# Two halves of weights taken together in up, gate and the first down, and other places for modulation rows 64 to 140

## The reference, cut to what matters

```
mod = silu(c) @ w_ada + b_ada                 # 6 slices of 2048: shift, scale, gate, twice
h = rms_norm(x, g) * (1 + scale_m) + shift_m
proj = h @ w_in                               # q, k, v, xs, z, b, c, dt
x = x + gate_m * (concat(attn, ssm) @ w_out)  # causal attention beside a state space mixer
h = rms_norm(x, g) * (1 + scale_f) + shift_f
u = causal_conv3(h @ w_up)                    # "up", 11264 columns
x = x + gate_f * ((silu(g) * val) @ w_down)   # "down", 5632 rows; then a final norm
# second block: norms, neighbourhood attention, latent attention, memory attention, and
x = x + (silu(h @ w_gate) * (h @ w_up)) @ w_down   # "gu" and "down2"
```

## Time and profile before

| | |
|---|---|
| median of 3 runs | 2675.37 us (2675.3 to 2676.28) |
| the profiled execution | 2672.84 us, its span 2670.9 us |
| mean granted TensorE clock | 0.996 of full |
| PE busy | 2625.8 us (98%) |
| POOL busy | 2197.8 us (82%) |
| ACT busy, DVE busy | 1252.9 us (47%), 1178.4 us (44%) |
| L1308 and L1313, PE busy | 833.8 us in 3328 matmuls, 464.7 us in 3328 matmuls |
| moved by DMA | 587.40 MB, 220 GB/s over the span |

### The profile page before, as it was taken

The page is one execution under the profiler, slowest core; times in us unless marked ns, Lnnn a source line. Parts: engine busy times, 40 slices in busy tenths (PEclk is TensorE's granted clock), DMA queues, the critical chain, the costliest instruction groups (busy, mean ns, idle before and its releaser), DMA issues.

```text
span 2670.9 us, 41760 instructions
## 1 busy us (share of the span) xinstructions
PE 2625.8 (98%) x16042; PEld 2349.0 (88%) x16042; DVE 1178.4 (44%) x1416; ACT 1252.9 (47%) x1496; POOL 2197.8 (82%) x889
## 2 busy tenths in 40 slices
PE   8999999999999999999999999999999999999998
PEld 8989998898888888888898888989998888888886
DVE  6777767774546464422364346722311111113223
ACT  5444454545444444444653454533544444444444
POOL 7878866787999998899898755866888888889997
PEclk9999999999999999999999999999999999999999
DMA  9998986674666665455455533634545555555553
GB/s 374 392 401 321 391 332 255 240 262 163 244 228 240 231 236 189 173 204 189 173 189 198 184 139 115 238 137 158 190 179 187 187 187 188 189 187 191 196 195 126
DMA packets 101760, 587.40 MB, mean 220 GB/s; under 512 B 11240, under 2 KB 13416, under 8 KB 45200
## 3 DMA queue, kind: packets, MB, share of 16 engines
q1 hardware_dynamic: 93600, 570.07, 57.7%
q10 hardware_dynamic: 8048, 15.74, 1.7%
HBM read 579.46 MB, written 8.40 MB: 220 GB/s over the span
## 4 chain that ended last, share of the span: by engine, by line
PE 85%; POOL 5%; DVE 4%; issue 3%; DMA 2%; ACT 1%; POOLq 0%; DVEq 0%; ACTq 0%; SPq 0%
PE ps L1308 29%; PE ps L1313 15%; PE ps L1325 6%; PE ps L1274 5%; PE ps L1267 5%; PE ps L1269 5%; POOL w_lo L547 5%; PE ps L1356 4%; PE ps L1358 4%; PE ps L1364 4%; PE ps L1330 3%; DMA arena<-ada 1%; DVE ps L2055 1%; PE ps L1631 1%; PE ps L1965 1%
## 5 line engine op out<-in xcount | busy, mean ns | idle before, releaser
L547 POOL TENSOR_TENSOR w_lo<-raw,w_hi 128x1024 fp32r<-128x1024 f32 x884 | 2197.4, 2500 | 455.2 <-ACT w_hi L570 452.5
L570 ACT CAST w_hi<-raw 128x1024 fp32r<-128x1024 f32 x884 | 924.3, 1051 | 1124.7 <-PE ps L1313 572.7
L1308 PE MATMUL ps<-a_both,w_hi 128*128 128x512 f32 x3328 | 833.8, 393 | 0.0
L1308 PEld LDWEIGHTS ps<-a_both,w_hi 128*128 128x128 f32 x3328 | 599.5, 189 | 106.1
L1313 PEld LDWEIGHTS ps<-a_both,w_lo 128*128 128x128 f32 x3328 | 454.0, 191 | 33.0 <-POOL w_lo L547 0.8
L1313 PE MATMUL ps<-a_both,w_lo 128*128 128x256 f32 x3328 | 464.7, 283 | 0.0
L1267 PE MATMUL ps<-a_both,w_hi 128*128 128x256 f32 x1616 | 404.9, 289 | 9.9 <-issue 3.3
L1269 PE MATMUL ps<-a_both,w_hi 128*128 128x256 f32 x1616 | 397.8, 284 | 0.0
L1267 PEld LDWEIGHTS ps<-a_both,w_hi 128*128 128x128 f32 x1616 | 311.7, 193 | 13.7 <-issue 4.8
L1269 PEld LDWEIGHTS ps<-a_both,w_hi 128*128 128x128 f32 x1616 | 312.0, 193 | 0.4
L2586 DVE TENSOR_TENSOR ps<-ps,work 128x1024 f32<-128x1024 f32 x42 | 51.8, 1232 | 505.9 <-ACT work L936 505.9
(11 more groups left out here) (262 smaller groups left out, 2034.6 us busy)
## 6 DMA issues: line engine op xcount, KB each, us to landing
raw<-stream SPq DMA_DIRECT2D x440, 1024.0 KB, 4.8
arena<-ada SPq DMA_DIRECT2D x185, 512.0 KB, 6.4
work<-ada SPq DMA_DIRECT2D x7, 512.0 KB, 7.1
arena<-memT SPq DMA_DIRECT2D x4, 512.0 KB, 10.0
res<-xT SPq DMA_DIRECT2D x4, 512.0 KB, 13.7
v_spill<-arena ACTq DMA_DIRECT2D x4, 512.0 KB, 3.4
k_spill<-arena ACTq DMA_DIRECT2D x4, 512.0 KB, 7.5
rel_rows<-rel_row ACTq DMA_DIRECT2D x4, 512.0 KB
```

Of the source, the lines that this page charges most:

```text
L547: pool.tensor_tensor(w_lo[:, h % SLOTS], raw_half(h), w_hi[:, h % SLOTS].bitcast(F32), ALU.subtract).then_inc(lo_ready, 1)
L570: act.copy(w_hi[:, base % 4], raw[:, tile_slot, (base % 2) * HALF:(base % 2 + 1) * HALF]).then_inc(hi_ready, 1)
L1308: pe.matmul(acc_two(g + turned)[:, f], w_hi[:, h % SLOTS, cols(k, f)], a_both[:, c0 + k], start=first and k == 0, stop=False, skip_group_c ...
```

## The change

It does two things that do not touch each other. `half_two` becomes `two_halves`: highs of half h, highs of half h + 1, then lows of h, lows of h + 1, with the same waits and the same count after each half's lows. Every caller goes in steps of two. The number of matmuls, weight loads and waits is the same. `ROW_POINTS` has other points between h = 62 and h = 140, so that VectorE's calls get these ends:

| call at h | 63 | 69 | 75 | 85 | 87 | 97 | 105 | 115 | 116 | 118 | 120 | 121 | 123 | 125 | 131 | 133 | 138 |
|---|---|---|---|---|---|---|---|---|---|---|---|---|---|---|---|---|---|
| rows until, before | 64 | 70 | 77 | 89 | 92 | 103 | 112 | 116 | 117 | 119 | 121 | 122 | 124 | 126 | 132 | 134 | 140 |
| rows until, after | 65 | 72 | 82 | 93 | 96 | 106 | 112 | 117 | 118 | 121 | 124 | 125 | 127 | 130 | 136 | 137 | 140 |

SyncE uses the same function, so that rows are issued behind other tiles: row 111 behind tile 54 and not 56, and rows 114 and 115 behind tile 56 and not 57.

```diff
--- before.py
+++ after.py
@@ -183,8 +183,8 @@
 
 
 
-ROW_POINTS = [(-1, 0), (3, 2), (58, 64), (62, 64), (66, 67), (92, 98), (105, 112), (111, 112), 
-              (138, 140), (146, 140), (164, 150), (168, 154), (176, 160), (186, 160)]
+ROW_POINTS = [(-1, 0), (3, 2), (58, 64), (62, 64), (66, 68), (69, 72), (75, 82), (92, 102), (103, 112), (111, 112),
+              (120, 124), (130, 136), (138, 140), (146, 140), (164, 150), (168, 154), (176, 160), (186, 160)]
 
 
 ADA_BACK = 150
@@ -1297,22 +1297,26 @@
                                        start=False, stop=last and k == 1, skip_group_check=True)
                 mm.then_inc(half_used, 1)
 
-            def half_two(h, g, c0, first, last, i=None, step=0, turned=0):
+            def two_halves(h, g, c0, first, last, i=None, step=0, turned=0):
 
                 def cols(k, f):
                     return slice(k * 512 + f * P, k * 512 + (f + 1) * P)
 
-                wait_high(h, i, step)
-                for k in range(2):
-                    for f in range(4):
-                        pe.matmul(acc_two(g + turned)[:, f], w_hi[:, h % SLOTS, cols(k, f)], a_both[:, c0 + k],
-                                  start=first and k == 0, stop=False, skip_group_check=True)
-                wait_half(h, i, step)
-                for k in range(2):
-                    for f in range(4):
-                        mm = pe.matmul(acc_two(g + turned)[:, f, 0, :], w_lo[:, h % SLOTS, cols(k, f)],
-                                       a_hi[:, c0 + k, :], start=False, stop=last and k == 1, skip_group_check=True)
-                mm.then_inc(half_used, 1)
+                for s in range(2):
+                    wait_high(h + s, i, step)
+                    for k in range(2):
+                        for f in range(4):
+                            pe.matmul(acc_two(g + turned)[:, f], w_hi[:, (h + s) % SLOTS, cols(k, f)],
+                                      a_both[:, c0 + 2 * s + k], start=first and s == 0 and k == 0, stop=False,
+                                      skip_group_check=True)
+                for s in range(2):
+                    wait_half(h + s, i, step)
+                    for k in range(2):
+                        for f in range(4):
+                            mm = pe.matmul(acc_two(g + turned)[:, f, 0, :], w_lo[:, (h + s) % SLOTS, cols(k, f)],
+                                           a_hi[:, c0 + 2 * s + k, :], start=False, stop=last and s == 1 and k == 1,
+                                           skip_group_check=True)
+                    mm.then_inc(half_used, 1)
 
             def half_pair(h, G, c0, first, last):
 
@@ -1344,8 +1348,8 @@
                 G, h0 = G0[name] + g, H0[name] + 8 * g
                 n = G // 2
                 pe.wait_ge(evac[G % 2], n if i is None else i + n)
-                for s in range(8):
-                    half_two(h0 + s, g, 2 * s, s == 0, s == 7, i, 16, int(name == "gu"))
+                for s in range(0, 8, 2):
+                    two_halves(h0 + s, g, 2 * s, s == 0, s == 6, i, 16, int(name == "gu"))
 
             def half_N(h, out2, c0, first, last, i=None, step=0):
 
@@ -1706,7 +1710,7 @@
                     G = G0["up"] + 20
                     pe.wait_ge(evac[G % 2], G // 2 + 1)
                     ada_sum(5, 0)
-                half_two(H0["up"] + 168 + s, 21, 2 * s, s == 0, s == 7)
+                two_halves(H0["up"] + 168 + s, 21, 2 * s, s == 0, s == 6)
 
             def down(name, hs0):
 
@@ -1731,7 +1735,8 @@
                         if first and kp == 0 and half == 1 and name == "down":
                             pe.wait_ge(evac[sets[cg]], (G + cg) // 2 + 1)
                         if name == "down":
-                            half_two(base_n + s, cg, par * 4 + 2 * kp, first and kp == 0, last and kp == 1, i, 8)
+                            if kp == 0:
+                                two_halves(base_n + s, cg, par * 4, first, last, i, 8)
                         else:
                             half_N(base_n + s, outs_tok[half][cg], par * 4 + 2 * kp, first and kp == 0,
                                    last and kp == 1, i, 8)
@@ -1765,9 +1770,7 @@
                             pe.wait_ge(mod_ready, len(ADA_ORDER))
                         for n in range(2):
                             pe.wait_ge(hl_ready, hs0 + n + 1)
-                            for kp in range(2):
-                                h = base + 4 * cg + 2 * n + kp
-                                half_two(h, cg, n * 4 + 2 * kp, n == 0 and kp == 0, False)
+                            two_halves(base + 4 * cg + 2 * n, cg, n * 4, n == 0, False)
 
                 for half in range(2):
                     n0 = 11 * half
```

## The result

The changed kernel takes 2687.02 us (median of 5 runs, 2685.24 to 2689.63) where the kernel before takes 2675.37 (5 runs): 1.0050 times as long, 95% interval 1.0038 to 1.0061, 11.6 us slower. The forecast was 2670.8 with a range to 2679; it was wrong in size and in sign. The profiled execution has a span of 2683.3 us, 12.4 more than before; it is the fastest of the five.

The account below looks back on a forecast made before the run. TensorE, busy 98% of the span, was taken as the bound, so only its waits or matmul pace could yield time. Pairs at -4.6 us and row terms summing to 0.0 turned 2675.37 into 2670.8 us, range 2659 to 2679.

Parts of the forecast that it names:

- Part one: Pairing halves in up, gu and down: each of 208 pairs saves 0.022 us net, -4.6 us.
- third rival: Order is free: pairing halves gains nothing and the row changes net 0, giving 2675.4 us; chance 0.12.
- I cost it at nothing: Later release of each pair's first half was priced at zero; 5.5 us over three places if the cover went.
- (a): Row 64 between two steps of the first norm, before the casts xs waits for: +0.5 us (0 to 1.3).
- (b): Three more rows and a fold before the second convolution of xs: +3.3 us, plus +1.7 for low clock.
- (c): TensorE's wait for VectorE at the dt sums disappears: -2.3 us (-2.3 to 0).
- (d): Seventh fold: row 111 issued sooner removes TensorE's wait, -2.4 us, and transposes stay at full clock, another -1.7.
- (f): Seventh pair of heads: one row less before `mixing` 13 removes the wait and its low clock, -3.9 us.
- (e): At the heads, more rows before `mixing` 5 make TensorE wait: +4.8 us (0 to +9.1).
- second rival: VectorE falls behind: at the heads more rows than fit between two pairs, +3.6 us, 2679.0 us; chance 0.13.

Follow-up runs that it names:

- experiment 8: Kernel before with two_halves and old row points, but up's last eight halves taken singly with half_two: 2667.82 us, 0.9981.
- experiment 5: Kernel before with the new row points only up to h = 87 (rows 64 to 96): 2676.64 us, 1.0011.
- experiment 6: Kernel before with row 111 one tile sooner and rows 130 and 131 ahead of `mixing` 11: 2667.90 us, 0.9980.
- 9: Kernel before with one row point edited, (105, 112) to (103, 112), putting rows 114 and 115 ahead of tile 57: 2679.21 us, 1.0020.
- experiment 1: Kernel before with two_halves alone, row points as before: 2671.46 us, 0.9993.
- experiment 10: Kernel before with new row points at 120 and 130 only, plus (116, 117) so row 116 stands behind `mixing` 2: 2680.01 us, 1.0024.
- experiment 3: Changed kernel, but SyncE issues rows 114 and 115 behind stream tile 57 again: 2679.85 us, 1.0026 against the kernel before.
- experiment 4: Kernel before with only the two new row points at 120 and 130, rows up to 112 as before: 2679.92 us, 1.0026.
- experiment 7: Kernel before with turned halves (highs h, lows h, lows h + 1, highs h + 1) in gu and up except its last group: 2669.31 us, 0.9987.
- experiment 2: Kernel before with the new row points alone, half_two as before: 2691.04 us, 1.0066.

## Why the prediction was wrong

**Part one, -4.6 forecast.** The pattern was right: a rise from 256 to 512 columns costs, a wait does not. In the kernel after only the first five of 16 highs are slow. A pair saves 0.020 us and not 0.022 (0.100 per five pairs, all through up and gu; the second low, too, is fast only behind a high, 0.119), so -4.2. The third rival, that the order is free, is out. The formula of the Trainium skill (TensorE: Matmul & The Clock Gate, Back-to-back issue gap) for the isolated gap of a matmul at full clock, columns over 2.4 GHz plus 2.5 ns, gives 216 and 109 ns for the two kinds (an estimate), and the same section has about 131 ns for 512 columns in a stream of weight loads and matmuls, which this is. The trace agrees with none of these figures: it has 227 and 120 in every kernel here. The failed step is "I cost it at nothing" for the later release. I looked only at the casts of w_hi and at w_lo in the first down. The cost came through other work in ScalarE's order, the casts of u, at the one place where a chain behind them ends on TensorE: 1.5 us, about the 1.85 us delay less the 0.5 us of room that L2087 had before; experiment 8, with single halves in that one group, has no such wait. A smaller slip: the 2.4 us for w_lo do not stand in the earlier trace rows, which have 2.8 each; with 2.8 the chain is 8.6 us and still far under 14.8.

**(a)** +0.5 forecast, 0.0 measured. With row 64 there TensorE waits 0.6 us for VectorE's L2136 and then 0.5 and not 1.1 us for ScalarE's cast; from matmul 1156 to 1300 the kernels before and after take the same time to 0.01 us.

**(b)** +5.0 forecast, measured +6.75, and +1.5 for w_lo ahead of it. The count of rows between the two convolutions was right, and so was the loss of the wait of 3.30 us. What failed is that I let the first convolution stand where it stood: two more rows now come before it as well (72 and not 70 at h = 69), one of which is waited for.

```profile
227.24 1.29 DVE L2058 SCALAR_TENSOR_TENSOR ps<-arena,small,ps 128x1024 f32<-128x1024 f32 x1 [3.54 <-DMA arena<-ada]
228.44 1.90 DVE L2277 TENSOR_SCALAR work<-ps,vec 128x256 f32<-128x256 f32 x4
...
255.28 1.89 DVE L2277 TENSOR_SCALAR work<-ps,vec 128x256 f32<-128x256 f32 x4
```

The first convolution starts at 228.44 and not 225.51, 2.9 us later, the second at 255.28 and not 248.54. And the tiles that stand behind these rows come late too: ScalarE's cast of the dt weights waits for one.

```profile
247.69 1.99 ACT L570 CAST w_hi<-raw 128x1024 fp32r<-128x1024 f32 x2 [3.94 <-DMA raw<-stream]
```

**(c)** -2.3 forecast, -2.4 measured. **(d)** -4.1 with the clock, -4.2 measured. But (d) was right in part by luck, and had more than the cause that I gave it: in experiment 5, with row 111 in its old place, TensorE's own lateness from (b) is enough to cover the whole wait; row 111 sooner by itself (6 and 9) shortens the wait by 0.6 and 1.6 us, and the clock's 1.5 us are gone in experiments 1, 8 and 10 too, where row 111 has its old place. Of (b), (c) and (d) together the kernel keeps +1.7. **(f)** -3.9, measured -3.9 (2.3 of wait, 1.6 of clock), and at the heads of experiment 6 it stands alone.

**(e)** +4.8 forecast, +16.6 measured, the step that decided the sign. Three things were wrong with it, and a further 2.4 us at 402 and 422 is the clock and a third wait for `mixing`. First, tile 57: the prediction saw it move behind rows 114 and 115 but priced it at its own 2.6 us of transfer; what counts is the wait of row 114 on SyncE's queue, 17.4 us long, which the tile now shares: +7.0 (experiments 3 and 9). Second, it named TensorE's demand at the pairs (L1551) only; the segment of head h + 2 needs `mixing` h too (L1534), so that `mixing` 2 behind row 116 costs 1.7 in the kernel after and 4.8 in experiment 4. Third, rows were sized at 2.26 us each; the eight rows from 116 to 123 took 20.9 us in the kernel after, 2.6 each, with 1.8 of waits for transfers, and `mixing` 5 came 5.4 us after TensorE was ready for it: +5.5. These eight rows took 17.1 us before, 14.9 in experiment 4 and 19.4 in experiment 10, and in experiment 1 the clock and a wait for `mixing` 5 cost 3.7 us with the row points of before: a mean per row could not size this term, and what sets the length of a row is open. The second rival, "VectorE falls behind", had the direction but only +9.1 for it, and gave (f) away, which stayed.

So the rival that ended slower was the nearest, with the same fault in its size. Its chance of 0.13 rested on a bound of +9.1 for (e), in which tile 57 stands with 2.6 us.

## What to carry to other kernels

A step that is moved on a queue is priced by the longest wait that it now shares, not by its own length: list for each queue the waits that are not its own business (here row 114's wait for Gram matrices), and check that nothing needed on another engine's in-order list crosses one. For a buffer released later, follow every in-order list that the release feeds to where it next meets the critical engine, also through work that does not use the buffer. An order of two kinds of work can be turned (a b, b a) and so have the gain of grouping without a later release.

## What had not been expected of the hardware

A wait of TensorE of one length is followed by a stretch at 1.2 GHz in one execution and not in another. Behind the wait for the seventh fold the clock fell after 2.35 us (before) and 3.00 (experiment 7), and did not after 2.84 (experiment 1), 2.72 (10) and 2.11 (8). Behind the wait of 2.2 us at the seventh pair it fell in the kernel before and in experiments 1, 7, 8 and 9, and did not in 5. The terms of 1.7 us for the clock in such sums are chances, not costs.

The stretch ahead of up was always 6.8 us, and the wait there always 5.4 us, but the stretch began 2.79 us ahead of the first matmul before and 1.53 after, so that TensorE was busy in it for 4.03 and 5.29 us: 0.5 us lost at the same wait, by the starts of matmuls, where the pairs win 1.7 in all of up. In experiment 3 it began 3.44 us ahead and in experiment 2 only 0.92, and up's first 58 matmuls took 1.1 us longer in the latter.
